# Six slots in place of four for the expert weights that are fetched ahead, and a semaphore for each piece

## The reference

```python
def clamped_swiglu_expert(xb, w_gu, b_gu, w_down, b_down):
    gu = xb @ w_gu + b_gu                       # 1024 -> 2048
    g, u = gu[:, :D_FF], gu[:, D_FF:]
    g = jnp.minimum(g, SWIGLU_LIMIT)
    u = jnp.clip(u, -SWIGLU_LIMIT, SWIGLU_LIMIT)
    h = (u + 1.0) * (g * jax.nn.sigmoid(SWIGLU_ALPHA * g))
    return h @ w_down + b_down                  # 1024 -> 1024
...
y = jnp.zeros((n, d)).at[slot_tok].add(yb * slot_w[:, None])
```

## Time and profile before

| | us |
|---|---|
| median of 3 runs | 2548.66 |
| lowest, highest | 2547.48, 2551.8 |
| profiled execution | 2544.7 |
| its span in the profile | 2542.7 |

### The profile page before, as it was taken

How to read it: one execution, slowest core, us unless ns; L and a number is a source line. 1 busy time by engine, 2 the same in 40 slices (tenths; PEclk the granted TensorE clock), 3 DMA queues, 4 the chain that set the end, 5 groups by cost and what they waited for, 6 DMA issues and landing times.

```text
span 2542.7 us, 31708 instructions
## 1 busy us (share of the span) xinstructions
PE 2369.2 (93%) x9597; PEld 1733.8 (68%) x9598; DVE 1550.6 (61%) x1526; ACT 1137.8 (45%) x1078; POOL 401.2 (16%) x344
## 2 busy tenths in 40 slices
PE   7998399989989968999999999999999999999995
PEld 4563274454464556888878888887887787887873
DVE  4536841101052368777776665777778787997783
ACT  4123111022032335565544544556557566774663
POOL 0361400000000001121211211212113022221211
PEclk9989659998999968999999999999999999999998
DMA  5002010130002138787977876879799889997894
GB/s 154 33 1 73 12 42 41 66 133 0 33 34 69 67 111 311 248 312 243 317 242 230 294 227 206 287 259 312 249 300 360 302 288 310 376 371 239 309 347 160
DMA packets 212946, 506.66 MB, mean 199 GB/s; under 512 B 19172, under 2 KB 19400, under 8 KB 211688
## 3 DMA queue, kind: packets, MB, share of 16 engines
q1 hardware_dynamic: 196912, 459.98, 50.4%
q0 software_dynamic: 14032, 45.77, 7.2%
q10 hardware_dynamic: 1960, 0.35, 0.1%
HBM read 469.62 MB, written 35.26 MB: 199 GB/s over the span
## 4 chain that ended last, share of the span: by engine, by line
PE 74%; DVE 9%; issue 5%; DMA 5%; ACT 5%; DVEq 1%; ACTq 0%; SPq 0%; POOLq 0%
PE PS L558 27%; PE PS L861 17%; PE PS L882 11%; PE PS L865 9%; PE PS L889 5%; DMA WA<-in_exp_w_down 4%; DVE WL L1647 2%; DMA WA<-in_exp_w_gu 1%; PE PS L914 1%; PE PS L853 1%; PE PS L818 1%; ACT WH L1165 1%; DVE H L1431 1%; ACT WA L952 1%; ACT YT L952 1%
## 5 line engine op out<-in xcount | busy, mean ns | idle before, releaser
L1647 DVE TENSOR_TENSOR WL<-WA,WH 128x2048 fp32r<-128x2048 f32 x384 | 877.1, 2289 | 302.0 <-ACT WH L1181 113.9
L861 PE MATMUL PS<-WH,XEH 128*128 128x512 f32 x1344 | 361.4, 391 | 0.0
L861 PE MATMUL PS<-WH,XEL 128*128 128x512 f32 x1344 | 361.1, 391 | 0.0
L865 PE MATMUL PS<-WL,XEH 128*128 128x512 f32 x1344 | 347.0, 390 | 0.0
L1165 ACT CAST WH<-WA 128x2048 fp32r<-128x2048 f32 x128 | 243.8, 1907 | 219.3 <-PE PS L865 143.4
L1160 ACT CAST WH<-WA 128x2048 fp32r<-128x2048 f32 x128 | 243.8, 1909 | 198.0 <-PE PS L865 151.5
L1181 ACT CAST WH<-WA 128x2048 fp32r<-128x2048 f32 x124 | 236.6, 1910 | 204.3 <-PE PS L889 181.7
L861 PEld LDWEIGHTS PS<-WH,XEL 128*128 128x128 f32 x1344 | 253.4, 189 | 53.3
L861 PEld LDWEIGHTS PS<-WH,XEH 128*128 128x128 f32 x1344 | 253.5, 189 | 52.1
L865 PEld LDWEIGHTS PS<-WL,XEH 128*128 128x128 f32 x1344 | 253.0, 188 | 52.8
L558 PE MATMUL PS<-WB,YT 128*128 128x512 f32 x512 | 222.9, 593 | 2.6 <-DVE YT L1261 1.6
(11 more groups left out here) (266 smaller groups left out, 2449.3 us busy)
## 6 DMA issues: line engine op xcount, KB each, us to landing
WA<-in_exp_w_gu SPq DMA_DIRECT2D x256, 1024.0 KB, 6.1
WA<-in_exp_w_down SPq DMA_DIRECT2D x128, 1024.0 KB, 7.0
WB<-in_xa_wkv SPq DMA_DIRECT2D x4, 2048.0 KB, 7.8
WB<-in_w_in SPq DMA_DIRECT2D x3, 2048.0 KB, 10.8
y_acc<-H SPq DMA_DIRECT2D x9, 512.0 KB, 2.6
H<-in_x SPq DMA_DIRECT2D x4, 1024.0 KB, 5.9
WB<-in_w_out SPq DMA_DIRECT2D x2, 2048.0 KB, 7.8
WA<-in_x SPq DMA_DIRECT2D x1, 4096.0 KB, 12.1
```

Of the source, the lines that this page charges most:

```text
L861: nc.tensor.matmul(PS[:, 2 * h + t, :], x[:, KT4 * half + k, t * P:(t + 1) * P], WH[:, j % 4, k * HALF:(k + 1) * HALF], start=False, stop= ...
L865: ins = nc.tensor.matmul(PS[:, 2 * h + t, :], XEH[:, KT4 * half + k, t * P:(t + 1) * P], WL[:, j % 4, k * HALF:(k + 1) * HALF], start=Fals ...
L1647: v.tensor_tensor(WL[:, s, :], RAW[:, s, :], WH[:, s, :].bitcast(F32), sub).then_inc(done, 1)
```

## The change

RAW gets six slots: four in WA, as before, and two in the first 4096 columns of H. The pieces take the six slots in turn in the order given above, so gate-up piece j has slot (j + 2) mod 6 and down piece m slot (m + 4) mod 6, the same in every iteration. SyncE's waits ahead of each transfer name the piece six before, in place of four. Each of the twelve pieces has a semaphore of its own that its transfer raises, in place of one for each slot and kind. BDN and GF3 go to other columns of H. To have semaphores left, some are joined: `d_in` into `par_in`, `mem_in` into `x_again`, `gb_in` into `rt_in` (whoever waits for one of them waits for all of the joined transfers), and `scatter_go` into `gather_go`, for which nobody waits. The computation is the same.

```diff
-        BDN = Hf[:, 0:D]
-        GF3 = Hf[:, 2048:2048 + L * 3 * E].rearrange("p (l e) -> p l e", l=L)
+        BDN = Hf[:, 4096:4096 + D]
+        GF3 = Hf[:, 5120:5120 + L * 3 * E].rearrange("p (l e) -> p l e", l=L)
...
         RAW = wa(0, 4, KT4 * HALF)
+        RAWH = Hf[:, 0:2 * KT4 * HALF].rearrange("p (s c) -> p s c", s=2)
+
+        def raw(s):
+            return RAWH[:, s, :] if s < 2 else RAW[:, s - 2, :]
+
+        def raw_gu(j):
+            return raw((j + 2) % 6)
+
+        def raw_dn(m):
+            return raw((m + 4) % 6)
...
-        rg_in = [sem(f"raw{s}_gu_in") for s in range(4)]
-        rd_in = [sem(f"raw{s}_dn_in") for s in range(4)]
+        rg_in = [sem(f"gu{j}_in") for j in range(8)]
+        rd_in = [sem(f"dn{m}_in") for m in range(4)]
...
-            sp.dma_start(DB, A["s5_d"].partition_broadcast(P)).then_inc(d_in, 16)
+            sp.dma_start(DB, A["s5_d"].partition_broadcast(P)).then_inc(par_in, 16)
...
                     for s in range(4):
-                        sp.wait_ge(gu_low, 8 * i + s + 1)
+                        if s < 2:
+                            sp.wait_ge(dn_low, 4 * i + s + 3)
+                        else:
+                            sp.wait_ge(gu_low, 8 * i + s - 1)
                         load_gate_up(4 + s, bass.ds(e_i, 1))
                 with sp.If_cmp(n_p, 0, "IS_GT"):
                     e_p = entry(sp, 0, i, E - 1)
                     for m in range(4):
                         with sp.If_cmp(n_i, 0, "IS_GT"):
-                            sp.wait_ge(gu_low, 8 * i + m + 5)
+                            sp.wait_ge(gu_low, 8 * i + m + 3)
                             load_down(m, bass.ds(e_p, 1))
                         with sp.Else():
                             sp.wait_ge(dn_low, 4 * i + m + 1)
                             load_down(m, bass.ds(e_p, 1))
                 with sp.If_cmp(n_n, 0, "IS_GT"):
                     e_n = item_expert(sp, i + 1)
-                    with sp.If_cmp(n_p, 0, "IS_GT"):
-                        for s in range(4):
-                            sp.wait_ge(dn_low, 4 * i + s + 5)
-                            load_gate_up(s, bass.ds(e_n, 1))
-                    with sp.Else():
-                        for s in range(4):
-                            sp.wait_ge(gu_low, 8 * i + s + 5)
-                            load_gate_up(s, bass.ds(e_n, 1))
+                    for s in range(4):
+                        if s < 2:
+                            sp.wait_ge(gu_low, 8 * i + s + 7)
+                        else:
+                            sp.wait_ge(dn_low, 4 * i + s + 3)
+                        load_gate_up(s, bass.ds(e_n, 1))
...
-                    act.wait_ge(rg_in[s], 32 * i + 32)
+                    act.wait_ge(rg_in[4 + s], 16 * i + 16)
                     act.wait_ge(gu_used, 8 * i + s + 5)
-                    nc.scalar.copy(WH[:, s, :], RAW[:, s, :]).then_inc(gu_high, 1)
+                    nc.scalar.copy(WH[:, s, :], raw_gu(4 + s)).then_inc(gu_high, 1)
```

More of the change, by code:

```diff
@@ L305, in build @@
         x_in = [sem(f"x_in{n}") for n in range(4)]
-        vec_in, par_in, blk_in, mem_in = sem("vec_in"), sem("par_in"), sem("blk_in"), sem("mem_in")
-        x_again, d_in, rt_in = sem("x_again"), sem("d_in"), sem("rt_in")
+        vec_in, par_in, blk_in = sem("vec_in"), sem("par_in"), sem("blk_in")
+        x_again, rt_in = sem("x_again"), sem("rt_in")
         w_in_s = [sem(f"wslot{s}_in") for s in range(2)]
@@ L331, in build @@
         ohr_done = sem("ohr_done")
-        acc_out, ids_done, gs_in, scatter_go = sem("acc_out"), sem("ids_done"), sem("gs_in"), sem("scatter_go")
+        acc_out, ids_done, gs_in = sem("acc_out"), sem("ids_done"), sem("gs_in")
         ms_done, itm_done, ite_done = sem("ms_done"), sem("itm_done"), sem("ite_done")
@@ L347, in build @@
             sem("y_done"), sem("y_out"), sem("ys_free"), sem("gather_go"), sem("moe_done"))
-        bias_high, gb_in, bias_zero = sem("bias_high"), sem("gb_in"), sem("bias_zero")
+        bias_high, bias_zero = sem("bias_high"), sem("bias_zero")
         bd_high, bd3_done, gt_high = sem("bd_high"), sem("bd3_done"), sem("gt_high")
@@ L457, in _ @@
                     sp.dma_start(XR0, x_tok).then_inc(x_again, 16)
-                    sp.dma_start(MEM, A["mem"].rearrange("b (m p) d -> p (b m) d", p=P)).then_inc(mem_in, 16)
+                    sp.dma_start(MEM, A["mem"].rearrange("b (m p) d -> p (b m) d", p=P)).then_inc(x_again, 16)
             wait_filled(sp, ("ot", NH - 1, 1, 1))
@@ L461, in _ @@
             sp.dma_start(RB, A["router_b"].partition_broadcast(P)).then_inc(rt_in, 16)
-            sp.dma_start(GB, A["norm_ffn_g"].partition_broadcast(P)).then_inc(gb_in, 16)
+            sp.dma_start(GB, A["norm_ffn_g"].partition_broadcast(P)).then_inc(rt_in, 16)
             for b in range(2):
@@ L478, in load_gate_up @@
                 f, h = divmod(u, 2)
-                sp.dma_start(RAW[:, j % 4, :].rearrange("p (k c) -> p k c", k=KT4),
+                sp.dma_start(raw_gu(j).rearrange("p (k c) -> p k c", k=KT4),
                              gu_v[:, e, half, :, h, f, :].rearrange("p e k c -> p (e k) c")) \
-                    .then_inc(rg_in[j % 4], 16)
+                    .then_inc(rg_in[j], 16)
             def load_down(m, e):
-                sp.dma_start(RAW[:, m, :].rearrange("p (k d) -> p k d", k=2),
+                sp.dma_start(raw_dn(m).rearrange("p (k d) -> p k d", k=2),
                              dn_v[:, e, m, :, :].rearrange("p e k d -> p (e k) d")).then_inc(rd_in[m], 16)
@@ L578, in _ @@
             transposes("xt", 0, YT)
-            pe.wait_ge(par_in, 16 * 6)
+            pe.wait_ge(par_in, 16 * 7)
             for w, u in enumerate((("cre",), ("cim",))):
@@ L777, in _ @@
                     if l == 0:
-                        pe.wait_ge(rt_in, 32)
+                        pe.wait_ge(rt_in, 48)
                     o = begin(("rl", l))
@@ L1068, in _ @@
                                                bias=V[:, V_GLB + cb:V_GLB + cb + 1]), u)
-            act.wait_ge(mem_in, 16)
+            act.wait_ge(x_again, 32)
             for m in range(MT):
@@ L1132, in _ @@
                 act.wait_ge(rg_in[j], 16)
-                nc.scalar.copy(WH[:, j, :], RAW[:, j, :]).then_inc(gu_high, 1)
+                nc.scalar.copy(WH[:, j, :], raw_gu(j)).then_inc(gu_high, 1)
             act.wait_ge(ohr_done, 1)
@@ L1164, in down_high @@
                     act.wait_ge(dn_used, 4 * i + m + 1)
-                    nc.scalar.copy(WH[:, m, :], RAW[:, m, :]).then_inc(dn_high, 1)
+                    nc.scalar.copy(WH[:, m, :], raw_dn(m)).then_inc(dn_high, 1)
                 def down_pair(m0):
@@ L1177, in next_high @@
                 def next_high(s):
-                    act.wait_ge(rg_in[s], 32 * i + 48)
+                    act.wait_ge(rg_in[s], 16 * i + 32)
                     act.wait_ge(gu_used, 8 * i + s + 9)
                     act.wait_ge(dn_used, 4 * i + s + 5)
-                    nc.scalar.copy(WH[:, s, :], RAW[:, s, :]).then_inc(gu_high, 1)
+                    nc.scalar.copy(WH[:, s, :], raw_gu(s)).then_inc(gu_high, 1)
                 def gate(half, tiles):
@@ L1355, in _ @@
             B0, B1 = BRW[:, 0, :, :], BRW[:, 1, :, :]
-            dve.wait_ge(par_in, 16 * 6)
+            dve.wait_ge(par_in, 16 * 7)
             tt(BB[:, 0], wide(S[6]), B0, mul)
@@ L1480, in _ @@
                 tt(y, y, SG[:, n % 2, :], mul, s=glu_done)
-            dve.wait_ge(x_again, 16)
+            dve.wait_ge(x_again, 32)
             for c in range(2):
@@ L1565, in _ @@
                     if n == 0:
-                        dve.wait_ge(gb_in, 16)
+                        dve.wait_ge(rt_in, 48)
                     stt(XR0[:, n, :], H[:, n, :], sm[:, n + 16:n + 17], GB, mul, mul, s=xn_done[3])
@@ L1573, in _ @@
                     v.tensor_tensor(BIASR[E:2 * E, :], BST[E:2 * E, :], BIASR[E:2 * E, :].bitcast(F32), sub).then_inc(bias_done, 1)
-                    dve.wait_ge(rt_in, 32)
+                    dve.wait_ge(rt_in, 48)
                     dve.wait_ge(iota_done, 4)
@@ L1644, in low_tokens, with low_weights @@
                 ins.then_inc(xel_done, 1)
-            def low_weights(s, done):
-                v.tensor_tensor(WL[:, s, :], RAW[:, s, :], WH[:, s, :].bitcast(F32), sub).then_inc(done, 1)
+            def low_weights(s, src, done):
+                v.tensor_tensor(WL[:, s, :], src, WH[:, s, :].bitcast(F32), sub).then_inc(done, 1)
             dve.sem_inc(dn_low, 8)
@@ L1653, in _ @@
                 dve.wait_ge(gu_high, j + 1)
-                low_weights(j, gu_low)
+                low_weights(j, raw_gu(j), gu_low)
                 if j == 0:
@@ L1675, in gate_up_low @@
                     dve.wait_ge(gu_high, 8 * i + j + 1)
-                    low_weights(j % 4, gu_low)
+                    low_weights(j % 4, raw_gu(j % 8), gu_low)
                 def down_low(m):
                     dve.wait_ge(dn_high, 4 * i + m + 1)
```

(6 more changed lines are left out.)

## The result

The changed kernel takes 2512.31 us (2511.99 to 2514.05), the kernel before on the same occasions 2550.23 (2547.48 to 2551.84): a ratio of 0.9854 with a 95% interval of 0.9837 to 0.9871, so 1.5% or 37 us less (the two medians themselves lie 37.9 us apart). The prediction was 2525.1 with a range from 2517 to 2538. The profiled executions are 32.3 us apart, 2544.7 and 2512.45 (spans 2542.7 and 2510.4).

What follows compares the result with a forecast made beforehand. TensorE, busy 93% of the span, was taken to bound the kernel. Gains of 4.8 + 2.4 + 6.1 + 6.1 + 4.5 = 23.9 us, less 0.3, gave 2548.7 - 23.6 = 2525.1 us; range 2517 to 2538.

Steps and rivals of the forecast that it cites:

- the five stretches: Parts of the expert loop, each beginning where a one-tile item follows a two-tile item; all TensorE stops, 23.5 us, fall there.
- Half clock: TensorE at 1.2 GHz after four stops, 1.7 us each, 6.7 us together, counted as lateness that slots absorb.
- But the transfers aren't made faster: Weight transfers stay at 3.04 us a piece; two more slots absorb only 6.1 us, once in each stretch.
- C: Third stretch of the expert loop, 119.6 us long: late weights cost 10.3 us, 6.1 gained, 4.2 kept.
- D: Fourth stretch of the expert loop, 190.0 us long: late weights cost 8.3 us, 6.1 gained, 2.2 kept.
- A: First stretch of the expert loop, 41.0 us long: late weights cost 4.8 us, all of it gained.
- B: Second stretch of the expert loop, 40.0 us long: late weights cost 2.4 us, all of it gained.
- E: Fifth stretch of the expert loop, 41.1 us long: late weights cost 4.5 us, all of it gained.
- all lateness goes: Rival, chance 0.18: in the loop, an earlier start of transfers saves more than two pieces; 30 us less, 2519 us.
- The ceiling of 30.3 us: Expert loop: the whole cost of late weights, stops plus half clock, about 30.3 us, the most the change can gain.
- The first item: Start of the loop: gu1 of the second item is issued about 6 us later; 0.3 us lost, bounds 0 and 3.4.
- Gathers and scatters: Rival, chance 0.05: queued weights delay the scatter into y_acc that POOL waits for in one-tile items; slower, 2579 us.

Runs made afterwards that it cites:

- e3: Kernel before, without TensorE's products with the weights' low parts and with VectorE making only 256 of 2048 columns of each low part; 2237.26 us.
- e4: Changed kernel, without TensorE's products with the weights' low parts and with VectorE making only 256 of 2048 columns of each low part; 2203.66 us.
- e5: Kernel before, only TensorE's products with the weights' low parts left out, VectorE making every low part whole; 2311.93 us.
- e6: Changed kernel, only TensorE's products with the weights' low parts left out, VectorE making every low part whole; 2271.51 us.
- e2: Changed kernel with six slots, but each transfer waits for the piece five before; 2519.28 us, ratio 0.9883 to the kernel before.
- e7: Kernel before, unedited, profiled a second time; span 2545.5 us.
- e8: Kernel before, unedited, profiled a third time; span 2547.2 us.
- e1: Changed kernel with six slots, but each transfer waits for the piece four before, as in the kernel before; 2548.26 us, ratio 0.9993.

## Why the prediction was wrong, point by point

**What bounds the kernel, and the place of the loss: right.** The 18 stops, 23.5 us, became eight of together 3.4 us, and the gain lies in the five stretches and nowhere else; ScalarE's waits for the down transfers went with them; two-tile items kept their times within 0.05 us. The chain from SyncE's issue of dn0 over ScalarE's wait to XEL was as described. Half clock behind the stops went too.

**"But the transfers aren't made faster": the step that failed.** The rate of three saturated items in the kernel before, 3.04 us a piece, was taken for the engines' limit because their busy share was 1.0 ("The engines can't carry that"). The runs put the limit at 383 GB/s (e3, e4), 35.65 us an item, 0.15 us above TensorE's 35.50, where the prediction had 0.73 (36.43 against 35.7). 374 GB/s was the ring of four, bound by its round trip of 12.1 us (shown by e5 against e6 and e3). What followed from that step, that C would keep 4.2 us and D 2.2, was wrong: C gave 10.8 in place of 6.1 and D 9.5 in place of 6.1. With A 4.0 (forecast 4.8), B 2.4 (2.4) and E 4.7 (4.5), the sum is 31.4 against 23.9. e2 shows it most plainly: five slots gave 30 us where the same arithmetic, used as the lower bound, gave 14.5. A, B and E, one item each, came out about as forecast. The late stops of 0.5 to 1 us that the prediction looked for in C and D aren't there: each keeps one of 0.49 us at XEL, in its first item.

The rival *all lateness goes*, at 0.18, named nearly the right outcome for the spans (its 30 us against 31.4 in the loop), and its condition was met at the heads of the stretches: dn0's 10.1 us were queueing behind scatters, and issued ahead of them it landed in 5.1. That reason covers the head items, whose gains are 4.0, 2.4, 4.9, 3.1 and 4.7 us, 19.1 of the 31.4. It doesn't cover the 12.2 us of the later items in C and D: there dn0 took 7.9 to 9.4 us before and takes 10 to 13 now, and those items are faster all the same. No run changes the order of scatters and weights alone, so how the heads' gain is shared between this and the slots isn't shown.

**The base: a term that was left at a difference.** The forecast put the gain of one profile under the median, and noted the 4 us between them without asking why. The losses of the kernel before differ from execution to execution (e7, e8), its 13 timed executions beside e1 and e2 lie between 2544.75 and 2553.04, and the profiled one was at the good end. The changed kernel has no such stretch in this part of its profile and varies less: 2511.99 to 2514.05. So the medians are 5.7 us further apart than the profiles. The ceiling of 30.3 us was one of the first profile, not of the kernel; by e1's it would have been 38. So the forecast missed by 12.8 us in two steps: the fixed rate cost 7.5 us of gain, and the base and what lies outside the five stretches the rest (5.7 for the base, 1.25 for the start of the loop, less 1.6 because the kernel before itself ran at 2550.23 this time and not at 2548.66). With the first alone put right, the forecast would have been 2517.6.

**The first item: no loss that shows.** Forecast was a loss of 0.3 us, bounds 0 and 3.4. The first two items take 73.6 us together, and 73.5 to 73.9 in the three profiles of the kernel before; e2, with five slots, takes 75.6. The stop of 4.65 us in it is the same to the hundredth, and ScalarE copied gu0 and gu1 of the second item without a gap:

```profile
981.22 3.70 ACT L1192 CAST WH<-WA 128x2048 fp32r<-128x2048 f32 x2
```

**Last item and merged semaphores: right, 0.** The stop before the last down pieces is 5.83 us in both; e1 has the rest of the change at a ratio of 0.9993.

**Gathers and scatters: right not to fear them.** The scatter landed after 9.3 us where it took 9.1, and GpSimd still waits 17.86 us behind it. The landing of a gate-up piece grew from 6.6 to 10.1 us at the same time, which is the longer queue seen from inside. How the 16 engines share their time between the two queues shows only in the 10.1 us at A given above, where both had work: 53 and 47%.

**Half clock: the size right, the use wrong.** The 1.7 us a stretch agree with the spans of e7 and e8 as far as these are explained; what was wrong was to count them as lateness that slots must absorb. Without the stop there is no such stretch, and C has neither of its two now.

## What to carry to other kernels

A DMA busy share of 1.0 doesn't say that the engines are at their limit: it was 1.02 at 367 GB/s (e5) and 1.04 to 1.05 at 383. The round trip of a slot over the number of slots doesn't say it either, since in a full ring it always gives the time that is seen: 12.1 / 4 in the kernel before, 11.9 / 4 in e3, which was at the limit. What told them apart was a run with less work behind the transfers: it rose to 383 GB/s with the same four slots. Before a rate is called a limit, make such a run; where the rate rises, the engines weren't at their limit, and one more slot can be worth more than the piece it stores, as in e2. And where short stops of TensorE bring half clock with them, look at how far the timed executions spread before a gain is taken from one profile.

## What the runs showed of the hardware

With three or more pieces of 1 MB under way on the average the transfers of this kernel ran at 382 to 383 GB/s, gathers and scatters included (the weights alone at 353 in the kernel after, 37.56 MB in 106.5 us), whether the ring had four slots (e3) or six (e4); the landing grew from 9.4 to 14.9 us between these two. With 2.3 under way they ran at 374 (the kernel before) and 367 (e5).

The Trainium skill ("DMA: Bandwidth & Descriptors", section Bandwidth) has about 358 GB/s as what binds loads from HBM, and says in the same section that this is a core's share when both cores of an HBM domain stream. The runs of this kernel, which uses one core, went beyond it, so they don't agree with the first sentence and don't test the second.

A weight transfer that was issued 1.6 us behind the second of two scatters landed after 10.0 us, and one issued 6.3 us ahead of the next scatter after 5.1 us (first item of A, before and after).

A stop of TensorE of 2.27 us in D was followed by half clock in e1 and not in the first profile of the kernel before, which has one of the same length there. The kernel before, with seven stops of 1.9 to 2.4 us in its first profile, lay between 2544.75 and 2553.04 us in 13 executions; the changed kernel, with none, between 2511.99 and 2514.05 in four.
